# Routed expert layers: block outputs go back to the tokens through DRAM and an indirect transfer instead of matmuls

## What is computed

```python
def hier_moe(x, w_rg, b_rg, w_re, b_re, w_gate, w_up, w_down):
    t = x.reshape(-1, D)
    g_val, g_idx = lax.top_k(softmax(t @ w_rg + b_rg), 1)       # one of 4 groups per token
    e_val, e_idx = lax.top_k(logits of the group's 4 experts, 2)  # two of its 4 experts
    combine = group_w[:, :, None] * within[:, None, :]
    for g in range(G):
        hg = silu(t @ w_gate[g]) * (t @ w_up[g])
        y = y + einsum('tef,efd->td', hg * combine[:, g, :, None], w_down[g])
```

## Time and profile before

| what | value |
|---|---|
| median of 3 runs | 1869.6 us (1868.13 to 1869.69) |
| the profiled execution's own time | 1869.45 us |
| its span in the profile | 1867.6 us |
| PE busy | 1838.9 us, 98% |
| DVE busy | 1174.8 us, 63% |
| ACT busy | 1122.3 us, 60% |
| POOL busy | 811.1 us, 43% |
| granted TensorE clock over the span | 0.999 of full |

### The profile page before, as it was taken

One profiled execution on the slowest core, in us unless ns is written; L12 is line 12 of the kernel. 1 busy time (PEld: TensorE's weight loads), 2 busy tenths in 40 slices (PEclk: granted clock), 3 DMA queues, 4 the chain that ended last, 5 costly groups with the idle time before them and its releaser, 6 DMA issues.

```text
span 1867.6 us, 32232 instructions
## 1 busy us (share of the span) xinstructions
PE 1838.9 (98%) x12426; PEld 1567.9 (84%) x12426; DVE 1174.8 (63%) x1635; ACT 1122.3 (60%) x1516; POOL 811.1 (43%) x403
## 2 busy tenths in 40 slices
PE   9999999999999999999999999999999999999998
PEld 8888989988888888898788888888888888888886
DVE  4332454866562433373224999999952689999997
ACT  5444656444364544443555878778764578778776
POOL 7988775531198888867684000000057420000000
PEclk9999999999999999999999999999999999999999
DMA  6555453310045655544447999999744599999993
GB/s 261 203 181 181 161 185 131 126 54 4 26 157 185 216 181 194 187 147 169 158 175 312 369 373 369 361 355 363 288 158 158 184 356 390 361 371 361 359 360 123
DMA packets 61187, 431.99 MB, mean 231 GB/s; under 512 B 6784, under 2 KB 7296, under 8 KB 10112
## 3 DMA queue, kind: packets, MB, share of 16 engines
q1 hardware_dynamic: 58176, 419.02, 60.3%
q10 hardware_dynamic: 1728, 6.95, 1.0%
q0 software_dynamic: 1152, 4.19, 0.6%
HBM read 426.99 MB, written 3.15 MB: 230 GB/s over the span
## 4 chain that ended last, share of the span: by engine, by line
PE 91%; DVE 5%; ACT 2%; issue 1%; POOL 0%; DMA 0%; SPq 0%; ACTq 0%; POOLq 0%; DVEq 0%
PE ps L838 20%; PE ps L812 11%; PE ps L1464 11%; PE ps L898 8%; PE ps L1421 8%; PE ps L1423 8%; PE ps L1422 7%; PE ps L1137 6%; PE ps L897 3%; PE ps L1446 1%; DVE w_low L2697 1%; PE ps L869 1%; PE ps L901 0%; ACT w_high L1674 0%; PE ps L951 0%
## 5 line engine op out<-in xcount | busy, mean ns | idle before, releaser
L724 POOL TENSOR_TENSOR w_low<-ring,w_high 128x1024 fp32r<-128x1024 f32 (+1 forms) x311 | 760.7, 2463 | 449.1 <-ACT w_high L1674 448.7
L1674 ACT ACTIVATE w_high<-ring 128x1024 fp32r<-128x1024 f32 (+1 forms) x480 | 502.0, 1057 | 411.5 <-PE ps L838 193.7
L2697 DVE TENSOR_TENSOR w_low<-arena,w_high 128x1024 fp32r<-128x1024 f32 x312 | 373.6, 1222 | 33.2 <-ACT w_high L1674 29.7
L1674 ACT ACTIVATE w_high<-arena 128x1024 fp32r<-128x1024 f32 x312 | 323.4, 1060 | 59.1 <-PE ps L1423 43.3
L838 PE MATMUL ps<-w_high,x_both 128*128 128x512 f32 (+1 forms) x1200 | 327.8, 389 | 1.6 <-ACT arena L1911 0.6
L838 PEld LDWEIGHTS ps<-w_high,x_both 128*128 128x128 f32 x1200 | 221.9, 188 | 48.6 <-issue 3.0
L1421 PE MATMUL ps<-w_high,x_both 128*128 128x512 f32 x640 | 254.1, 397 | 0.2
L1423 PE MATMUL ps<-w_high,x_both 128*128 128x512 f32 x640 | 249.9, 390 | 0.0
L1422 PE MATMUL ps<-w_low,x_both 128*128 128x512 f32 x640 | 249.3, 389 | 0.0
L812 PE MATMUL ps<-x_both,w_high 128*128 128x256 f32 x1264 | 239.8, 288 | 1.8 <-DVE w_low L2288 1.4
L898 PE MATMUL ps<-x_both,w_high 128*128 128x512 f32 x640 | 221.4, 396 | 0.0
(11 more groups left out here) (331 smaller groups left out, 2213.2 us busy)
## 6 DMA issues: line engine op xcount, KB each, us to landing
ring<-in_stream SPq DMA_DIRECT2D x239, 1024.0 KB, 4.8
arena<-in_stream SPq DMA_DIRECT2D x156, 1024.0 KB, 6.8
arena<-in_gains ACTq DMA_DIRECT2D x4, 512.0 KB, 4.1
normed_rows<-arena ACTq DMA_DIRECT2D x4, 512.0 KB, 9.8
con<-in_consts ACTq DMA_DIRECT2D x1, 1280.0 KB, 7.5
con<-in_consts SPq DMA_DIRECT2D x1, 1248.0 KB, 15.0
x<-in_x SPq DMA_DIRECT2D x2, 512.0 KB, 4.1
ring<-in_stream SPq DMA_DIRECT2D x2, 512.0 KB, 8.0
```

The costliest lines, as they stand in the source:

```text
L724: nc.gpsimd.tensor_tensor(w_low[:, t % AHEAD, 0:w], slot(SLOT[t // 2])[:, t % 2 * TW:t % 2 * TW + w], w_high[:, t % AHEAD, 0:w].bitcast(F3 ...
L1674: nc.scalar.activation(w_high[:, t % AHEAD, 0:w], slot(SLOT[c])[:, t % 2 * TW:t % 2 * TW + w], ACT.Copy)\
L2697: nc.vector.tensor_tensor(w_low[:, t % AHEAD, :], slot(SLOT[c])[:, t % 2 * TW:t % 2 * TW + TW], w_high[:, t % AHEAD, :].bitcast(F32), ALU. ...
```

## The change

Blocks 0 to 3 no longer pass through `scatter`. ACT copies their output to `block_out` in SBUF and stores it to a new DRAM tensor `block_rows` (512 rows) from its own DMA queue, one unit later (`store_out`). DVE computes each token's row there (group times 128 plus slot) in four small operations, into `token_row`. When all four blocks are stored, POOL fetches a row for each token with two indirect DMAs, one per 128 tokens, the second after the first has landed (`fetch_back`). After `hidden(18)` DVE adds them to `x` in two operations (`add_back`); the mask `near` is 0 for overflow tokens. Block 4 keeps its matmuls (`scatter_overflow`), and the transposes of `slots` fall from 10 to 2.

```diff
+            def fetch_back(l):
+                pool.wait_ge(gathered, 2 * BLOCKS * (l + 1))
+                pool.wait_ge(tokens_known, 2 * l + 2)
+                pool.wait_ge(rows_stored, 16 * STORES * (l + 1))
+                for tok in range(NT):
+                    pool.wait_ge(rows_fetched, 16 * (FETCHES * l + GROUPS + tok))
+                    nc.gpsimd.indirect_dma_start(
+                        out=fetched[:, tok, :], out_offset=None, in_=block_rows,
+                        in_offset=bass.IndirectOffsetOnAxis(ap=token_row[:, tok:tok + 1], axis=0))\
+                        .then_inc(rows_fetched, 16)
...
-                            pe.wait_ge(out_low, 2 * (BLOCKS * l + b))
+                            pe.wait_ge(out_high, 2 * (BLOCKS * l + b))
...
-                    up(u, [0, 1, 2])
-                    if j == 0:
-                        scatter(b - 1)
-                    up(u, [3])
+                    up(u, range(4))
...
+                        if b and half == 0 and b < BLOCKS - 1:
+                            act.wait_ge(rows_stored, 16 * (STORES * l + NT + b))
+                        whole = outs_high if b == BLOCKS - 1 else block_out
+                        nc.scalar.activation(whole[:, half * 512:half * 512 + 512], wk[2 + half], ACT.Copy)\
                             .then_inc(out_high, 1)
+                def store_out(b):
+                    act.wait_ge(out_high, 2 * (BLOCKS * l + b) + 2)
+                    act.dma_start(block_rows[b * P:b * P + P, :], block_out).then_inc(rows_stored, 16)
...
-                        for n, t in ((0, x_high), (1, x_low)):
-                            nc.scalar.activation(t[:, 2:4, :], acc[n].rearrange("p (b t) -> p b t", t=T), ACT.Copy)\
-                                .then_inc(slots_copied, 1)
-                        nc.scalar.activation(last_toks, acc[2][:, 0:T], ACT.Copy).then_inc(slots_copied, 1)
+                        nc.scalar.activation(overflow_toks, acc[0][:, 0:T], ACT.Copy).then_inc(slots_copied, 1)
...
+                    if j == 1 and b:
+                        store_out(b - 1)
...
+                op(TT(score, first_group, ids.unsqueeze(1).broadcast_to((P, NT, GROUPS)), ALU.mult))
+                op(nc.vector.tensor_reduce(total, score, AX.X, ALU.add))
+                op(STT(out=total, in0=total, scalar=float(P), in1=slot_pos, op0=ALU.mult, op1=ALU.add))
+                dve.wait_ge(tokens_known, 2 * l + 1)
+                nc.vector.tensor_copy(token_row[:, :], total).then_inc(tokens_known, 1)
...
+                def add_back(tok):
+                    dve.wait_ge(rows_fetched, 16 * (FETCHES * l + GROUPS + tok + 1))
+                    own.did(STT(out=x[:, tok, :], in0=fetched[:, tok, :], scalar=near[:, tok:tok + 1], in1=x[:, tok, :],
+                                op0=ALU.mult, op1=ALU.add))
...
-                    if j == 0:
-                        low_to(t0 + DOWN_AT[u - 1] + 3 + AHEAD)
-                        low_out(b - 1)
                     hidden(u)
+                    if u == LAST - 1:
+                        for tok in range(NT):
+                            add_back(tok)
```

More of the change, by code:

```diff
@@ L362, in settle, with two_blocks @@
         self.eng.wait_ge(self.sem, self.n)
-def two_blocks(nc, stream, params, consts, x_in, gate_bias, gains, normed_rows, out):
+def two_blocks(nc, stream, params, consts, x_in, gate_bias, gains, normed_rows, block_rows, out):
     ctx = ExitStack()
@@ L627, in two_blocks @@
         scratch = A(7)[:, 0:256]
-        last_toks = A(7)[:, 256:256 + T]
+        block_out = A(7)[:, 512:512 + D]
         outs_high, outs_low = (t[:, 4:8, :].rearrange("p k t -> p (k t)") for t in (x_high, x_low))
@@ L793, in _ @@
             fetch_rows(1)
+            fetch_back(1)
         @block.tensor
@@ L1397, in gather @@
                     if b:
-                        pe.wait_ge(rows_fetched, 16 * ((BLOCKS - 1) * l + b))
+                        pe.wait_ge(rows_fetched, 16 * (FETCHES * l + b))
                         for k in range(4):
@@ L1485, in down_by_half, with scatter_overflow @@
                             mm.then_inc(last_half, 1)
[L1487 to L1494, removed]
+                def scatter_overflow():
+                    pe.wait_ge(slots_copied, l + 1)
                     for half in range(2):
                         cols = slice(half * 512, half * 512 + 512)
-                        pe.wait_ge(out_low, 2 * (BLOCKS * l + b) + half + 1)
+                        pe.wait_ge(out_low, 2 * l + half + 1)
                         for tok in range(NT):
                             n = 2 * tok + half
[L1500 to L1505, removed]
+                            pe.matmul(acc[n], overflow_toks[:, tok * P:tok * P + P], outs_high[:, cols],
+                                      start=True, stop=False)
+                            pe.matmul(acc[n], overflow_toks[:, tok * P:tok * P + P], outs_low[:, cols],
+                                      start=False, stop=True).then_inc(acc_done if n < 3 else moe_summed, 1)
                 gather(0, 0, wk[0])
@@ L1511, in s_moe @@
                 pe.wait_ge(overflow_known, l + 1)
-                for b in range(BLOCKS):
-                    for tok in range(NT):
-                        mm = pe.transpose(accf[:, b * T + tok * P:b * T + tok * P + P], slots[:, tok, b, :], ident)
+                for tok in range(NT):
+                    mm = pe.transpose(acc[0][:, tok * P:tok * P + P], slots[:, tok, BLOCKS - 1, :], ident)
                 mm.then_inc(slots_turned, 1)
@@ L1547, in s_moe @@
                 down_by_half(LAST)
-                scatter(BLOCKS - 1)
+                scatter_overflow()
             def s_moba():
@@ L2836, in low_turned, with low_out @@
                         .then_inc(expert_low, 1)
-                def low_out(b):
+                def low_out():
                     for half in range(2):
-                        dve.wait_ge(out_high, 2 * (BLOCKS * l + b) + half + 1)
+                        dve.wait_ge(out_high, 2 * (BLOCKS * l + BLOCKS - 1) + half + 1)
                         cols = slice(half * 512, half * 512 + 512)
@@ L2872, in s_moe @@
                 low_to(t1)
-                low_out(BLOCKS - 1)
+                own.settle()
+                low_out()
                 for n in range(1, 4):
```

19 lines of the change are left out of this document (9 added, 10 removed).

## The result

The changed kernel takes 1857.28 us (median of 4 runs, 1856.62 to 1857.73). The kernel before took 1869.44 beside it (median of 4). The ratio is 0.9936 with a 95% interval of 0.9924 to 0.9947, so 12.2 us are gained; 10.8 were forecast. The profiled execution's own time is 1857.73 us, its span 1855.9, the mean granted clock 0.998.

The account below looks back on a forecast made before the run. PE, never idle in a block, was taken to set the pace, with DVE and the DMAs close behind. Terms of -7.27 + 0.7 - 0.35 + 1.5 gave -5.4 us per layer, -10.8 for two: 1858.8 us, range 1852.4 to 1865.0.

Parts of the forecast that it names:

- four scatters: Four of five scatters per layer go, each eight matmuls 0.227 us apart on PE: -7.27 us per layer.
- transposes of slots: Routing stage: eight of ten go, but PE then waits longer at turn(0) for hidden(0): 0 of 1.0 us gained.
- four small operations: DVE's token_row operations ahead of hidden(0), for which PE already waits: +0.7 us per layer, all on the path.
- ACT's copies: Two 128x512 copies that make w_high late go, only a 128x256 copy stays: -0.35 us per layer, bounds 0 and -0.35.
- additions to x: Two DVE additions, 2.57 us, between hidden(18) and two tiles, make PE stall: +1.5 us per layer, bounds 1.1 and 2.6.
- late rows, full DMA: Transfers: store and two fetches hidden by 2.8 us at the medians, DMA engines keep up with the weights: cost 0.
- Breathing space: Rival: without the scatter DVE lacks slack, each of eight units stalls PE by 0.5 us: 1862.8 us; chance 0.11.
- Slow additions: Rival: additions behind hidden(18) run slower than their row, the pair costs 1.3 us more per layer: 1861.4 us; chance 0.06.
- DMA full: Rival: 367 GB/s is the DMA ceiling, blocks take 71.4 us, 3.2 behind PE: 1862.0 us at most; chance 0.03.
- All hidden: Rival: everything added is hidden, transposes count too, additions cost nothing: -8.6 us per layer, 1852.4 us; chance 0.05.
- Late rows: Rival: fetched rows reach add_back late, DVE waits, PE runs dry: 1864.2 us if 2.7 late, 1875.4 if 8.3; chance 0.11.

Follow-up runs that it names:

- scatters back: Changed kernel with the eight matmuls of each scatter of blocks 0 to 3 run again at their old place, without low_out: 1871.36 us, ratio 1.0014.
- no traffic: Changed kernel without the four stores per layer and the two fetches back, DVE still doing both additions: 1856.26 us, ratio 0.9934.

## Why the prediction was right

**The sum.** Per layer, from the starts of `turn`:

| term | forecast | measured | from |
|---|---|---|---|
| four scatters | -7.27 | -7.2 to -7.3 | scatters back: +1.81 each; the kernel before without them: -1.81 each |
| transposes of slots | 0 | 0 | first transpose to `turn(0)`: 12.16 with ten, 12.18 with two |
| four small operations | +0.7 | +0.70 | `turn(0)`; gone when moved |
| ACT's copies | -0.35 | -0.41 (put back: +0.54) | `turn(0)` to `turn(1)` |
| additions to x | +1.5 | +1.41 | left out |
| late rows, full DMA | 0 | 0 | no wait at L2863; no traffic: same time |
| no term | | -0.65 | the other units, up to `turn(18)` |
| sum | -5.4 | -6.2 | |

From `turn(0)` to `turn(18)` it took 314.28 us before and takes 305.95 now, 8.33 less; with +0.70 and +1.39 at the two ends that is -6.24 per layer, -12.5 for two, against 12.2 between the medians.

The mechanism was right, and each named term came within 0.1 us. One zero was right for a reason that was not. The prediction let the time of the missing transposes go into a longer wait at `turn(0)`. It goes into the waits of 0.38 and 0.30 us for `w_low` in `up(0)`, where DVE sets the pace of the routing. Of the 0.41 of the copies, 0.35 is the pause of the earlier trace rows, and 0.06 is what other units gained too.

**The term that was missing** is the 0.65 us. Units without a scatter take 17.25 us where they took 17.31, and 16.79 where they took 16.81. In the units of 16.8 us it lies in the twelve matmuls between `turn` and `down`, whose starts are 0.23 us apart and here and there 0.24; those of 17.3 us lose about as much again behind the transposes of `gather`. The scatter matmuls are not its cause: left out of the kernel before, they leave 17.31 and 16.81; put into the changed one, 17.25. Nor are the transposes with the copies, the stores and fetches, or the additions: each of these put back or left out alone stays at 17.25. What is left, `low_out` and the buffers in which the matrices and outputs lie, was not tried, so its cause stays open.

**The rivals.** *Breathing space* is refuted: even with `low_out` in the unit, PE does not wait. *Slow additions* are refuted by the four L2863, 1278 ns each on average, and with them the rule of half throughput that the prediction took from the Trainium skill, Vector Engine (DVE) Microarchitecture Reference, Points that are easy to get wrong:

```profile
L2863 DVE SCALAR_TENSOR_TENSOR x<-arena,x 128x1024 f32<-128x1024 f32 x4 | 4.9, 1278 | 0.0
```

The row of the same shape was the right one to price them by. The other one there, 964 ns for 508 columns, was a mean of two cases. Its four instructions in the first part of the kernel before, and the POOL tiles beside the last two:

```profile
334.62 0.69 DVE L2456 SCALAR_TENSOR_TENSOR arena<-arena 128x508 f32<-128x508 f32 x1 [0.51 <-DVE arena L2448]
343.96 0.69 DVE L2456 SCALAR_TENSOR_TENSOR arena<-arena 128x508 f32<-128x508 f32 x1
352.10 1.47 DVE L2456 SCALAR_TENSOR_TENSOR arena<-arena 128x508 f32<-128x508 f32 x1
360.34 1.01 DVE L2456 SCALAR_TENSOR_TENSOR arena<-arena 128x508 f32<-128x508 f32 x1
...
350.62 2.41 POOL L724 TENSOR_TENSOR w_low<-ring,w_high 128x1024 fp32r<-128x1024 f32 x1 [0.80 <-ACT w_high L1674]
...
358.40 2.40 POOL L724 TENSOR_TENSOR w_low<-ring,w_high 128x1024 fp32r<-128x1024 f32 x1 [0.73 <-ACT w_high L1674]
```

With POOL idle it takes 0.69 us. Beside a tile of POOL it ends 0.54 and 0.55 us behind that tile's end, as L2201 does. So the trace of the kernel before already held the warning that an addition on POOL would slow DVE. *DMA full* is refuted by the kernel without traffic. *All hidden* did not happen: both small costs are on the path. *Late rows* did not come up, but were near. The chain was 26.3 us in the first layer (27.0 forecast) and had 4.2 to spare (2.8 forecast). The store's issue does not stand behind the end of `silu(17)`, as I had it, but at its start. One unit later, the chain made the kernel slower than the one before. There the price was wrong in form: the prediction let lateness go straight to PE, and 6.3 and 6.4 us of it cost 9.0 and 7.5, by the clock.

## What to carry to other kernels

Where PE is never idle, price removed matmuls by the distance of their starts, and then look for the places at which another engine is waited for: there a 0.16 us operation costs its pitch in full, and moved by one unit it costs nothing. A long operation belongs where its engine idles anyway. That another engine is idle is not enough: on POOL the additions cost 3.7 us per layer instead of 1.4, by what they did to DVE's tiles. Before pricing an operation by the mean of a row, look at its single instructions and at what ran beside them. Before making a transfer hang on the last moment, count its chain and its slack in microseconds: here it had 4.2 us to spare in the first layer, and issued one unit later it turned a gain of 12 us into a loss, as far as one run tells.

## What was not expected of the hardware

- DVE and POOL: five w_low tiles on DVE took 7.90 and 8.83 us beside POOL's arithmetic and 5.76 alone, and POOL's 128x512 TENSOR_SCALAR took 3.6 us beside them. A DVE TENSOR_SCALAR that takes 0.75 us alone took up to 2.39 and ended 0.54 to 0.56 us after POOL's tile, whatever came before; a SCALAR_TENSOR_TENSOR that takes 0.69 alone took up to 1.47 in the same way.
- After PE had stood still for 7.25 us its granted clock was 0.50, the 1.2 GHz level, for the next 5.5 us, with matmul starts 0.43 us apart; after 7.31 us in the other layer the starts were 0.23 apart again within 3.0 us. After waits of 0.75 and 0.93 us the clock stayed at 1.00.
- The indirect fetch of 128 rows landed in 8.5 to 9.2 us amid the weight stream (421 GB/s) and in 5.0 to 7.4 when issued one unit later, towards the stream's end in the layer (200 GB/s in the first).
